# Odd mixer of a two-block model on one core: 24 taps of one convolution tile on GpSimd, attention heads between slot halves, norm sums inside the output slots, and gate values in four column groups

## The reference, cut to what matters

```python
gates = (jnp.einsum('bhne,rheg->rbng', q, wq_g) + jnp.einsum('bhne,rheg->rbng', k, wk_g)
         + jnp.einsum('bhne,rheg->rbng', v, wv_g))
```

```python
p = x @ w_in                                  # q, k, v, forget gate, two halves of a gated unit
y_c = forgetting_attention(q, k, v, log_f)    # logits + cumulative log forget, softmax, times v
h = p_d[..., :D_D] * jax.nn.sigmoid(p_d[..., D_D:])
h = causal_dwconv(h, dw_w) + dw_b             # 31 taps, each channel for itself
y_d = jax.nn.silu(layer_norm(h, cn_g, cn_b))
return jnp.concatenate([y_c, y_d], axis=-1) @ w_out
```

## Time and profile before

| | us |
|---|---|
| median of 3 runs (1409.45 to 1410.57) | 1409.85 |
| the profiled execution's own time | 1408.28 |
| its span, first to last instruction | 1406.5 |
| PE busy | 1282.5 (91%) |
| DVE busy | 806.7 (57%) |
| ACT busy | 577.4 (41%) |
| POOL busy | 187.5 (13%) |

### The profile page before, as it was taken

One profiled execution on the slowest core, in us unless ns is written; L12 is line 12 of the kernel. 1 busy time (PEld: TensorE's weight loads), 2 busy tenths in 40 slices (PEclk: granted clock), 3 DMA queues, 4 the chain that ended last, 5 costly groups with the idle time before them and its releaser, 6 DMA issues.

```text
span 1406.5 us, 23032 instructions
## 1 busy us (share of the span) xinstructions
PE 1282.5 (91%) x9496; PEld 1182.6 (84%) x9496; DVE 806.7 (57%) x1208; ACT 577.4 (41%) x874; POOL 187.5 (13%) x147
## 2 busy tenths in 40 slices
PE   5899999999976789899998989999989966999997
PEld 2799877779963579899998989999989956999996
DVE  2767833336446667654436676555467886655544
ACT  2332433335541323444235435444345544544433
POOL 1242300044440001000200040111000000011100
PEclk9799999999988899999999999999999988999999
DMA  9557211114540004455133543555533303354551
GB/s 392 229 203 276 69 60 60 61 60 150 180 149 1 0 31 154 162 186 187 42 126 134 190 142 130 181 184 186 196 120 132 139 31 106 134 180 179 181 186 52
DMA packets 27473, 195.55 MB, mean 139 GB/s; under 512 B 3193, under 2 KB 3329, under 8 KB 3969
## 3 DMA queue, kind: packets, MB, share of 16 engines
q1 hardware_dynamic: 26496, 191.90, 37.9%
q10 hardware_dynamic: 896, 2.50, 0.5%
HBM read 193.33 MB, written 1.05 MB: 138 GB/s over the span
## 4 chain that ended last, share of the span: by engine, by line
PE 79%; DVE 12%; ACT 4%; issue 1%; POOL 0%; ACTq 0%; DVEq 0%
PE ps L398 23%; PE ps L400 23%; PE ps L399 23%; PE ps L440 3%; PE ps L603 3%; DVE acc L1863 2%; DVE w_lo L1365 2%; PE ps L537 1%; PE ps L540 1%; DVE V L1602 1%; ACT w_hi L848 1%; PE ps L455 1%; DVE xconv L1467 1%; DVE rstd L1672 1%; DVE wexp L1605 1%
## 5 line engine op out<-in xcount | busy, mean ns | idle before, releaser
L1365 DVE TENSOR_TENSOR w_lo<-ring,w_hi 128x1024 fp32r<-128x1024 f32 x292 | 362.2, 1250 | 336.2 <-ACT w_hi L848 335.7
L848 ACT ACTIVATE w_hi<-ring 128x1024 fp32r<-128x1024 f32 x312 | 327.3, 1058 | 493.0 <-PE ps L400 414.8
L398 PE MATMUL ps<-x_hi,w_hi 128*128 128x256 f32 x1216 | 349.8, 288 | 20.2 <-DVE x_lo L1681 20.2
L399 PE MATMUL ps<-x_lo,w_hi 128*128 128x256 f32 x1216 | 348.5, 287 | 0.0
L400 PE MATMUL ps<-x_hi,w_lo 128*128 128x256 f32 x1216 | 348.2, 286 | 0.0
L398 PEld LDWEIGHTS ps<-x_hi,w_hi 128*128 128x128 f32 x1216 | 238.1, 196 | 22.5 <-issue 22.5
L399 PEld LDWEIGHTS ps<-x_lo,w_hi 128*128 128x128 f32 x1216 | 238.3, 196 | 0.0
L400 PEld LDWEIGHTS ps<-x_hi,w_lo 128*128 128x128 f32 x1216 | 238.0, 196 | 0.0
L398 PE MATMUL ps<-g_hi,w_hi 128*128 128x256 f32 x608 | 171.9, 283 | 7.8 <-DVE g_lo L1989 4.9
L400 PE MATMUL ps<-g_hi,w_lo 128*128 128x256 f32 x608 | 171.7, 282 | 0.0
L399 PE MATMUL ps<-g_lo,w_hi 128*128 128x256 f32 x608 | 170.8, 281 | 0.0
(11 more groups left out here) (294 smaller groups left out, 2098.6 us busy)
## 6 DMA issues: line engine op xcount, KB each, us to landing
ring<-in_weights SPq DMA_DIRECT2D x156, 1024.0 KB, 4.9
o_sb<-in_weights SPq DMA_DIRECT2D x10, 1024.0 KB, 6.4
z_sb<-in_weights SPq DMA_DIRECT2D x10, 1024.0 KB, 6.8
V<-in_weights SPq DMA_DIRECT2D x3, 1024.0 KB, 22.2
dft<-in_dft ACTq DMA_DIRECT2D x1, 1026.0 KB, 5.3
X<-in_x SPq DMA_DIRECT2D x1, 1024.0 KB, 4.9
ctx_room<-in_ctx SPq DMA_DIRECT2D x1, 1024.0 KB, 7.3
xconv<-in_weights SPq DMA_DIRECT2D x1, 1024.0 KB, 27.3
```

Of the source, the lines that this page charges most:

```text
L398: mm(dst, w_h, x_h, start=start, stop=False, skip_group_check=True)
L399: mm(dst, w_h, x_l, start=False, stop=False, skip_group_check=True)
L848: do(w_hi[:, q % 2, part], ring[:, q % RING, part], ACT.Copy).then_inc(S("hi_ready"), 1)
L1365: v.tensor_tensor(w_lo[:, q % 2, part], ring[:, q % RING, part], w_hi[:, q % 2, part], ALU.subtract).then_inc(S("lo_ready"), 1)
```

## The change

- Gate values of v (PE): the 4 matmuls of a head write to four groups of 32 PSUM partitions (columns of the array), three with 32-column weights and one with 16. `gates` becomes 128 partitions high, and a new 128x16 matrix gate_fold, which DVE makes at the start by two small instructions, replaces fold_gates.
- POOL does taps 0 to 23 of the convolution's tile 3: one tensor_scalar for tap 0, then for each of 23 taps a tensor_scalar into `gated` and a tensor_tensor that adds it, in the order of one chain (47 instructions). It also does `lo` of odout slots 2 and 3.
- DVE does tiles 0, 1 and 2 together, tile 2 by two taps behind, then waits for POOL's 47 steps and does tile 3's taps 24 to 30 among the last of the others. `lo` of odout slot 1 comes after that. The splits of attention tiles 0 and 1 come amid the taps, those of 2 and 3 after the centring.
- PE issues logits as heads 0 to 2 after slot 6, 3 after slot 7, 4 to 6 after slot 8, 7 after slot 9. attend and turn of heads 0 and 1 go between the halves of odin slot 9, those of 4 and 5 and the mean sum between the halves of odout slot 0, attend 6 and 7 and the variance sum before slot 1. The sums go to PSUM banks 2 and 3.
- ACT's list is put in the matching order.

The core of the diff:

```diff
+POOL_TAPS = 24
+        gate_fold = sa("gate_fold", (P, 16))
-        gates = V[0:32, KE + 2, :]
+        gates = V[:, KE + 2, :]
+        conv_mean, conv_var = ps[:, 2, 0:SEQ], ps[:, 3, 0:SEQ]
 ...
                 for e in range(HC):
-                    last = mm(ps[0:16, 7, :], gate_w[:, 2 * KE + HC * hd + e, :], xm[e], start=False,
-                              stop=(hd == HEADS - 1 and e == HC - 1), skip_group_check=True)
+                    g = (e + 1) % HC
+                    n = 32 if g else 16
+                    last = mm(ps[32 * g:32 * g + n, 7, :], vcol("gate_w", (2 * KE + HC * hd + e) * 16, n), xm[e],
+                              start=(hd == 0 and g > 0), stop=(hd == HEADS - 1), skip_group_check=True)
 ...
             def odd_in(t, u, s, half):
+                if half == 1 and t == N_ODIN - 1:
+                    for hd in range(2):
+                        attend(hd)
+                        turn(hd + 2)
 ...
-                if t >= 6:
-                    logits(2 * (t - 6))
-                    logits(2 * (t - 6) + 1)
+                for hd in ((0, 1, 2), (3,), (4, 5, 6), (7,))[t - 6] if t >= 6 else ():
+                    logits(hd)
 ...
+                    if t == 0 and half == 1:
+                        for hd in range(4, 6):
+                            attend(hd)
+                            turn(hd + 2)
+                        pe.wait_ge(S("probT_moved"), 7)
+                        column_sum(conv_mean, ones_h[:, :], lambda k: acc31[:, k, :], KH, S("norm_in"),
+                                   S("norm_mean"), since("in", "conv"))
 ...
             mixed_slot(0)
-            for hd in range(4, FH):
+            for hd in range(6, FH):
                 attend(hd)
+            column_sum(conv_var, ones_h[:, :], lambda k: sq[:, k, :], KH, S("norm_squares"),
+                       S("norm_var"), since("squares", "conv"))
             mixed_slot(1)
 ... (POOL, between the two feed-forward parts)
+            pool.wait_ge(S("odin_moved"), KH)
+            chain.step(nc.gpsimd.tensor_scalar(conv3, last_pad[:, 2:2 + SEQ], vcol("dw_w", KH - 1),
+                                               vcol("dw_b", KH - 1), ALU.mult, ALU.add))
+            for k in range(1, POOL_TAPS):
+                product = gated[:, k % 2, :]
+                if k >= 3:
+                    chain.join(1)
+                chain.step(nc.gpsimd.tensor_scalar(product, last_pad[:, k + 2:k + 2 + SEQ],
+                                                   vcol("dw_w", k * KH + KH - 1), None, ALU.mult))
+                chain.join()
+                chain.step(pair_op(conv3, conv3, product, ALU.add))
+            for q in range(STARTS["odout"] + 2, STARTS["odout"] + 4):
+                pool.wait_ge(S("lo_ready"), 2 * q)
+                lo(q)
 ... (DVE)
+            def convolved(k0, k1):
                 for k in range(k0, k1):
-                    taps(k, pair)
+                    taps(k, (0, 1))
+                    if k >= 3:
+                        taps(k - 2, (2,))
 ...
+            convolved(28, TAPS - 1)
+            dve.wait_ge(S("pool_order"), 2 * POOL_TAPS - 1)
+            late = range(POOL_TAPS, TAPS - 1)
+            for k in late:
+                if k > late[2]:
+                    chain.join()
+                taps(k, (3,))
+                if k in late[:2]:
+                    taps(TAPS - 3 + k - POOL_TAPS, (2,))
+                if k - POOL_TAPS in (2, 3, 4):
+                    final_tap(k - POOL_TAPS - 2)
+            chain.join()
+            final_tap(3)
             lo(STARTS["odout"] + 1)
```

More of the change, by code:

```diff
@@ L559, in _ @@
                     pe.wait_ge(S("scores_moved"), HEADS)
-                last = mm(ps[0:4, (6, 7, 4, 5)[g], :], cc("fold_gates", 4 * g, 4 * g + 4)[0:32], gates, start=True, stop=True)
+                last = mm(ps[0:4, (6, 7, 4, 5)[g], :], gate_fold[:, 4 * g:4 * g + 4], gates, start=True, stop=True)
             last.then_inc(S("grow_done"), 1)
@@ L794, in _ @@
                     turn(1)
-            for hd in range(4):
+            for hd in range(2, 4):
                 attend(hd)
@@ L1400, in _ @@
             v.tensor_tensor(fold[:, :], fold[:, :], ident[:, 96:128], ALU.add).then_inc(S("fold_ready"), 1)
+            dve.wait_ge(S("fold_ready"), 1)
+            chain.step(v.tensor_copy(gate_fold[:, :], fold[:, 0:16]))
+            chain.join()
+            chain.step(v.tensor_tensor(gate_fold[0:32, :], gate_fold[0:32, :], fold[0:32, 16:32], ALU.add))
             dve.wait_ge(S("root_0"), 1)
@@ L1874, in first_tap, with final_tap, split_attention @@
                                            vcol("dw_b", t), ALU.mult, ALU.add))
[L1876 to L1881, removed]
+            def final_tap(t):
+                v.scalar_tensor_tensor(acc31[:, t, :], pad_a[:, t, TAPS + 1:TAPS + 1 + SEQ],
+                                       vcol("dw_w", (TAPS - 1) * KH + t), acc31[:, t, :],
+                                       ALU.mult, ALU.add).then_inc(S("norm_in"), 1)
+            def split_attention(c):
+                dve.wait_ge(S("attn_rounded"), c + 1)
+                for b in range(2):
+                    part = slice(FD * b, FD * (b + 1))
+                    ins = v.tensor_tensor(g_lo[part, KH + c, :], ps[part, c % 2, SEQ * b:SEQ * (b + 1)],
+                                          g_hi[part, KH + c, :], ALU.subtract)
+                    if b == 0:
+                        chain.step(ins)
+                ins.then_inc(S("attn_split"), 1)
             def maximum(hd):
@@ L1923, in _ @@
                 .then_inc(S("cum_ready"), 1)
+            convolved(10, 11)
             lo(STARTS["odin"] + 7)
-            convolved(15, 19, (0, 1))
+            convolved(11, 14)
             lo(STARTS["odin"] + 8)
[L1927 to L1932, removed]
+            convolved(14, 16)
+            for hd in range(3):
+                maximum(hd)
             lo(STARTS["odin"] + 9)
-            convolved(25, 27, (0, 1))
@@ L1935, in _ @@
-            maximum(2)
+            for hd in range(3):
+                sum_inverse(hd)
+            convolved(16, 18)
             maximum(3)
-            convolved(27, 29, (0, 1))
-            sum_inverse(2)
+            convolved(18, 19)
+            lo(STARTS["odout"])
+            convolved(19, 20)
+            maximum(4)
             sum_inverse(3)
[L1940 to L1943, removed]
             maximum(5)
-            for t in (2, 3):
-                first_tap(t)
@@ L1968, in _ @@
-            convolved(24, TAPS - 1, (2, 3))
-            final_tap((2, 3))
-            lo(STARTS["odout"] + 2)
+            convolved(21, 22)
+            sum_inverse(6)
+            convolved(22, 24)
+            split_attention(0)
+            convolved(24, 25)
+            maximum(7)
+            convolved(25, 26)
+            sum_inverse(7)
+            convolved(26, 28)
+            split_attention(1)
+            convolved(28, TAPS - 1)
+            dve.wait_ge(S("pool_order"), 2 * POOL_TAPS - 1)
@@ L1972, in _ @@
             for k in range(KH):
-                v.tensor_tensor(acc31[:, k, :], acc31[:, k, :], mean_ps, ALU.subtract)\
+                v.tensor_tensor(acc31[:, k, :], acc31[:, k, :], conv_mean, ALU.subtract)\
                     .then_inc(S("norm_centred"), 1)
-            lo(STARTS["odout"] + 3)
+            for c in range(2, KH):
+                split_attention(c)
             dve.wait_ge(S("norm_root"), since("root", "conv") + 1)
```

93 lines of the change are left out of this document (44 added, 49 removed).

## The result

The changed kernel takes 1390.16 us, the median of four runs (1389.23 to 1390.78), against 1410.12 for the kernel before, timed with it: a ratio of 0.986, with a 95% interval of 0.985 to 0.9875. A second timing, beside the experiments, gave 1388.42 against 1409.92 (0.985, 0.9836 to 0.9863). So it is faster by 20 to 21.5 us; I had forecast 7. The profiled execution took 1390.78 us with a span of 1388.9, where I expected a span of 1399.4.

A forecast was written before the change was run, and what follows sets the result against it. PE bounds the kernel nearly everywhere, but DVE's taps bound the odd mixer. Odd mixer 2.2 + 1.0 = +3.2 and gates -10.3 give -7.1: from 1409.85 to 1402.7 us, range 1391 to 1411.

The forecast's parts named there:

- Gates: Stage qk: v's four gate matmuls on four column groups take 0.96 us, saving 2.57 a head, 10.3 in all.
- DVE's own list: Odd mixer, from tile 3's pad to the last tap: DVE's work sums to 56.3 us, plus 5 of waits.
- PE's hole: Odd mixer: PE's 9.8 us wait for the transposes' moves, to be filled by heads between slot halves.
- T: Time of the last tap's signal in the odd mixer: forecast 1161.9, 2.2 later than before.
- The overlap of POOL and DVE: Odd mixer: POOL's 39.1 us delay DVE except where they overlap, 13.4 us at least, putting T at 1157 to 1166.8.
- The two rows at the ends of my range: Traces pricing POOL's delay to DVE: 4.1 us for two tensor_tensors in stage xm, 0.24 beside a tensor_scalar.
- The tail: From T to mix1's first sum: forecast 26.1 us against 25.1, 1.0 later, range -1 to +3.
- The old 4.9 of waiting: Tail: PE's 4.9 us wait for the split of the norm's output would be covered by slot 1.
- The free port: Rival, 15%: POOL's work in the odd mixer costs DVE nothing, T 1141.1 to 1150; with 1141.1, 1382 us.
- POOL shut out: Rival, 12%: DVE's tap stream keeps POOL out until DVE waits for it, T 1180.2, kernel 1421 us.
- my own case's signs: Likeliest case, 62%, 1397.8 to 1407.6 us: POOL busy well over 39 us, DVE waiting for POOL, last tap near 1151.6.
- The column groups: Rival, 8%: the gate matmuls' four groups don't run side by side; only the odd mixer's +3.2 stays, 1413 us.

The follow-up runs named there:

- a_gates: The kernel before with only v's gate values in four column groups: 1398.2 us, 11.9 below the kernel before.
- d_dve: The changed kernel with taps 0 to 23 of tile 3 given back to DVE: 1387.29 us, 2.9 below the changed kernel's first timing.
- b_odd: The changed kernel with the gate change undone: 1400.57 us, 9.5 below the kernel before.
- h_lo: d_dve with POOL doing the two lo halves of the last odin slot: stretch from pad 3 to the last tap's signal 70.38 us, against 69.87.

## Why the prediction was wrong

**Gates: right.** 0.99 us a head where I said 0.96, and 2.55 saved a head, 10.2 in all (10.3). DVE's wait shrank to 5.23 and stayed. But at pad 3 the changed kernel was only 7.7 us ahead: the head start was 9.7 at the last copy of scores (308.38 and 298.68) and shrank behind it, where the granted clock from 320 to 520 us was 0.89 (0.90 before). That a_gates won 11.9 says that this is no steady loss, and the same code's times to the pad differ by more.

**DVE's own list: right.** 56.3 forecast, 55.81 with POOL idle. Its waits were 8.0 and not 5, within my 2 to 9. But 2.5 of the 8.0 are for PE, where I had written that PE would be there by then. The heads between slot halves did not fill PE's hole: 6.8 us of waiting stand there in place of 9.8. It cost T nothing in the changed kernel, as DVE has no such wait in it.

Set beside the kernel before, DVE's list is where the odd mixer's gain comes from, with no help of POOL. The busy table of before for the same stretch, to be set beside d_dve's above:

```profile
1079.84:1159.69 79.85, 65.87 (x488) 62.72 (x486) 68.97 (x168) 44.83 (x104) 0.00 (x0) 0.91 0.27 93
```

All taps are on DVE in both; its work ahead of T falls by 3.8 (one slot's lo and two splits now lie behind T) and its waits by 6.2 (10.9 to 4.7): 10.0 of 10.0 us. The largest wait of before that is gone is this one, for ACT's rounding of an attention tile:

```profile
DVE g_lo L1963 <- ACT g_hi L1214: 4.6, 1, 4.6
```

That it is gone by the new order of heads, slots and taps is argued; no run takes one of the moves alone. Of the 10.0 the taps on POOL took 1.8 back and the shorter tail added 1.5, which together is the 9.5 of b_odd but for 0.2.

**The overlap of POOL and DVE: the step that failed.** I had the mechanism and mis-sized it. The sum took POOL's 39.1 us as exclusive but for 13.4 to 23 that would overlap, so that T would be 16 to 25.7 late on DVE's list. Measured, POOL's work takes 11.9 us of DVE's time, and 4.1 of those fall into its waits, so T moved by 7.85. The two rows at the ends of my range were both read rightly but carried over wrongly. The first was a tensor_tensor of 1024 columns, which does hold DVE off for its length (h_lo confirms it); I used it for instructions of 256, where the free part weighs. The second, the 0.24 of a tensor_scalar, was the nearest row for half of POOL's list, and it was even too high (0.10); I used it for 15 of the 24 only and took half of what it gave, and allowed the tensor_tensors no overlap of their own. The Trainium skill (SBUF — State Buffer, SBUF: two separate sides) has the pair of ports that both engines share held for the whole instruction, and the other engine fully blocked. The runs agree for long tensor_tensors (4.19 of 4.99), and not for the others: 0.42 of 0.74 and 0.10 of 0.92. So T was 71.67 us behind the pad, against 82.1 in my sum: 10.4 us less, by far the largest error: 13 us less for POOL's work (7.85 against 20.8), less 2.5 that DVE's own list with its waits was longer.

**The tail: 23.65, not 26.1.** Term by term: the mean 0.7 (1.0), the second half of slot 0 3.0 (5.1), heads 6 and 7 1.3 (1.2), the variance 1.5 (1.9), slots 1 to 3 17.1 (16.9). The error is the half slot: I gave its matmuls the low clock's 0.21, but PE had begun the sums of the first tiles 2.4 us ahead of T and came to the slot at the full clock, 0.12 a matmul. The prediction was not at one with itself here: its 8.6 us of work behind T are right only with the half slot at the full clock (5.7 and 2.9). The old 4.9 of waiting is covered, as forecast.

The terms close: pad 3 came 2.6 later than by my sum (7.7 in place of 10.3 earlier), the stretch 10.4 shorter, the tail 2.4 shorter, the rest 0.3: -10.5, from 1399.4 to 1388.9.

**The rivals.** The free port had T at 61.3 behind the pad and 1382 us; POOL shut out had it at 100. The truth is 71.7, half way between my forecast of 82.1 and the free port; counted by what POOL's work added to the stretch (7.85 of the 20.8 forecast) it is nearer to the latter. The free port's sign came true: POOL was done before DVE asked. Of my own case's signs two did as well, POOL busy for over 39 us and taps far above 0.48 (one took 0.94), and three did not: DVE did not wait for POOL, the last tap came at 1143.84 and not near 1151.6, and PE was not at half the clock behind the mean sum. So a long busy time of POOL was a poor sign, as a POOL instruction that stands for 12.6 us costs DVE nothing for most of it. The column groups do run side by side.

## What to carry to other kernels

Ask of an instruction that can keep another engine off what it takes from that engine, not how long it lasts: form and size decide it, so a row of the same form and of nearly the same size is needed, and two rows that disagree by a factor of four are a reason to price each form apart. Before work is given to POOL for relief, set that price beside what the work costs on DVE: here a tap is 0.10 + 0.42 us of DVE's time on POOL, in the mean of the stretch, and 0.40 on DVE itself. And look first for waits that ready work could fill: two moved blocks of taps shortened the stretch by 2.2 us, taking all of POOL's taps back by 1.8.

## What the runs showed that I had not expected

- POOL's long instruction beside DVE's stream is mostly waiting: 12.63 us of a 0.92 us tensor_scalar, with 18 DVE taps and two slots' lo at full speed beside it. One more pause per k cut it to 5.61.
- DVE's maxima, which read PSUM, pay nothing while POOL works: the 16 reduces of the eight heads take 4.87 us beside POOL and 4.89 without.
- Four fp32 matmuls (eight records) of 512 columns on four column groups take 1.06 us, on one they took 3.61, with one of the groups 16 columns wide.
- The same stretch of the odd mixer repeats to 0.06 us from execution to execution, while the 1070 us ahead of it differ by up to 4.8: a stretch is the finer measure of an edit.
